# From expert 12 on, down matrices through ScalarE's DMA queue, gate and up together through SyncE's

## The reference

```python
DEPTH = 2; SEQ = 256; D_MODEL = 1024; EXPERT_FF = 512; N_EXPERTS = 32
for l in range(DEPTH):
    h = rms_norm(x, norm_mix[l])
    mix = ...
    x = x + mix
    x = x + hierarchical_moe(rms_norm(x, norm_ffn[l]), ...)
...
def hierarchical_moe(x, ...):
    combine = ...
    for e in range(N_EXPERTS):
        h = jax.nn.silu(t @ w_gate[e]) * (t @ w_up[e])
        out = out + combine[:, e:e + 1] * (h @ w_down[e])
```

## Time and profile before

| what | value |
|---|---|
| median of 3 runs | 1071.91 us (1071.45 to 1071.99) |
| the profiled execution | 1072.4 us, span 1070.7 us |
| PE busy | 809.2 us (76%) |
| DVE, ACT busy | 315.5 us (29%), 194.5 us (18%) |
| HBM read | 437.84 MB, 410 GB/s over the span |
| 36 transfers of 6144 KB | median 33.8 us from issue to landing |

### The profile page before, as it was taken

How to read it: one execution, slowest core, us unless ns; L and a number is a source line. 1 busy time by engine, 2 the same in 40 slices (tenths; PEclk the granted TensorE clock), 3 DMA queues, 4 the chain that set the end, 5 groups by cost and what they waited for, 6 DMA issues and landing times.

```text
span 1070.7 us, 30243 instructions
## 1 busy us (share of the span) xinstructions
PE 809.2 (76%) x13948; PEld 643.4 (60%) x13949; DVE 315.5 (29%) x784; ACT 194.5 (18%) x363; POOL 5.4 (1%) x26
## 2 busy tenths in 40 slices
PE   9999978764867666776899999896456767666675
PEld 9788756543645545555599987564344545545453
DVE  5775522110111111111278744231111111111122
ACT  6784111000000000000254331110000000000002
POOL 1000000000000000000000000000000000000000
PEclk9999999887898888888999989998879888888888
DMA  9979999999999999999998599999999999999995
GB/s 368 425 300 415 388 426 427 428 442 427 428 434 435 424 432 439 433 430 422 418 428 356 218 415 408 425 428 428 439 438 425 422 435 437 433 428 432 441 417 241
DMA packets 26820, 439.94 MB, mean 411 GB/s; under 512 B 3200, under 2 KB 3712, under 8 KB 9088
## 3 DMA queue, kind: packets, MB, share of 16 engines
q1 hardware_dynamic: 26464, 438.36, 96.6%
q10 hardware_dynamic: 288, 0.54, 0.1%
HBM read 437.84 MB, written 1.05 MB: 410 GB/s over the span
## 4 chain that ended last, share of the span: by engine, by line
DMA 53%; PE 41%; issue 4%; DVE 1%; SPq 1%; ACT 1%; DVEq 0%; ACTq 0%
DMA ring<-in_expert_weights 51%; PE psum L1621 12%; PE psum L1409 8%; PE psum L1630 5%; PE psum L1481 4%; PE psum L1638 3%; PE psum L1649 3%; PE psum L1461 2%; DMA ring<-in_even_w_in 2%; PE psum L1644 1%; PE psum L1394 1%; PE psum L1746 1%; PE psum L1381 0%; PE psum L1532 0%; PE psum L1517 0%
## 5 line engine op out<-in xcount | busy, mean ns | idle before, releaser
L1621 PE MATMUL psum<-ring,m 128*32 128x128 f32 x7936 | 299.5, 319 | 225.6 <-DMA ring<-in_expert_weights 201.4
L1621 PEld LDWEIGHTS psum<-ring,m 128*32 128x32 f32 x7936 | 276.1, 130 | 257.8 <-issue 171.9
L1271 DVE TENSOR_TENSOR m<-psum,m 128x128 f32<-128x128 f32 x64 | 18.7, 292 | 544.5 <-ACT m L798 526.9
L1630 PE MATMUL psum<-ring,m 128*32 128x256 f32 x1984 | 120.5, 381 | 3.7 <-DMA ring<-in_expert_weights 3.7
L798 ACT ACTIVATE m<-psum 128x128 f32<-128x128 f32 x60 | 16.7, 278 | 495.2 <-PE psum L1621 495.2
L1409 PE MATMUL psum<-scr_halves,ring_halves 128*128 128x256 f32 x736 | 99.3, 284 | 0.8 <-DVE scr_halves L920 0.6
L1409 PEld LDWEIGHTS psum<-scr_halves,ring_halves 128*128 128x128 f32 x736 | 94.1, 192 | 1.7 <-issue 0.9
L1630 PEld LDWEIGHTS psum<-ring,m 128*32 128x32 f32 x1984 | 64.5, 111 | 49.6 <-issue 5.3
L1638 PE MATMUL psum<-m 32*128 32x256 f32 x1024 | 78.3, 408 | 15.3 <-issue 13.2
L1649 PE MATMUL psum<-x,m 128*32 128x256 f32 x1024 | 73.1, 404 | 1.4 <-issue 1.4
L1638 PEld LDWEIGHTS psum<-m 32*128 32x128 f32 x1024 | 48.1, 186 | 33.3 <-issue 27.6
(11 more groups left out here) (196 smaller groups left out, 518.0 us busy)
## 6 DMA issues: line engine op xcount, KB each, us to landing
ring<-in_expert_weights SPq DMA_DIRECT2D x36, 6144.0 KB, 33.8
ring<-in_expert_weights SPq DMA_DIRECT2D x68, 2048.0 KB, 23.9
ring<-in_expert_weights SPq DMA_DIRECT2D x16, 1024.0 KB, 11.1
ring<-in_odd_w_in SPq DMA_DIRECT2D x5, 2048.0 KB, 26.3
ring<-in_even_w_in SPq DMA_DIRECT2D x3, 2048.0 KB, 22.2
ring<-in_even_w_out SPq DMA_DIRECT2D x2, 2048.0 KB, 31.4
spare<-in_expert_weights SPq DMA_DIRECT2D x2, 2048.0 KB, 21.6
ring<-in_last_down SPq DMA_DIRECT2D x8, 512.0 KB, 32.9
```

The lines of the kernel that those rows point to most:

```text
L1621: last = pe.matmul(GU[CAP * part:CAP * (part + 1), lo:lo + FP], block_of(k), w_of(k)[:, FP * part:FP * (part + 1)], start=k == 0, stop=k = ...
L1630: last = pe.matmul(YB[CAP * part:CAP * (part + 1), 0:DP], h[:, CAP * f:CAP * (f + 1)], w[:, f, DP * part:DP * (part + 1)], start=f == 0, s ...
```

## The change

The transfer of a whole expert is cut in two. SP loads gate and up, 4096 KB, and waits for `gu_ready` of the expert three before, no longer for `y_ready`. ACT issues down, 2048 KB, behind its copy of `yy` of the expert three before; its loop over the turns is cut into four so that only the turns that have a successor to load do so (9 to 14 before `more_experts`, 15 to 26 after it). PE waits for the down matrix before the down product. 18 experts in each of two layers are loaded so.

```diff
--- before.py
+++ after.py
@@ -84,6 +84,7 @@
     for expert in range(FINE):
         if expert != EARLY:
             SINGLE += [entry(layer, expert) + mat for mat in range(3)]
+    SINGLE += [entry(layer, expert) + 2 for expert in range(FINE, NE - 2)]
     SINGLE += [entry(layer, NE - 2) + mat for mat in range(3)]
     SINGLE += [entry(layer, NE - 1) + mat for mat in range(2)]
 SINGLE.append(L_GAIN)
@@ -438,8 +439,9 @@
             def whole(l, e, i, former):
 
                 at = third(l, (i - 1) % TRI)
-                sp.wait_ge(y_ready, after(l, former))
-                sp.dma_start(ring[:, SLOT * 3 * at:SLOT * 3 * (at + 1)], expert_weights_in[l, e]).then_inc(whole_landed[at], 16)
+                sp.wait_ge(gu_ready, after(l, former))
+                sp.dma_start(ring[:, SLOT * 3 * at:SLOT * (3 * at + 2)],
+                             expert_weights_in[l, e][:, 0:2 * SLOT]).then_inc(whole_landed[at], 16)
 
             def turns(l, start, stop):
                 with sp.Fori(start, stop) as b:
@@ -801,6 +803,12 @@
                 act.wait_ge(y_ready, after(l, e))
                 act.activation(yy, YB[:, 0:DP], ACT.Copy).then_inc(yy_ready, 1)
 
+            def load_down(l, e, i):
+
+                n = entry(l, FINE + i) + 2
+                act.dma_start(tall(n), expert_weights_in[l, e][:, 2 * SLOT:3 * SLOT].rearrange("p (j d) -> p j d", j=4)) \
+                    .then_inc(landed[place(n)], 16)
+
             def last_experts(l):
                 for e in LAST_TWO:
                     act.wait_ge(gu_ready, after(l, e))
@@ -821,11 +829,13 @@
                                           scale=rstd[:, t:t + 1])
                 last.then_inc(exps_ready, 1)
                 preload(ACT.Silu)
-                for start, stop in ((0, MIDDLE), (MIDDLE, TURNS)):
+                for start, stop in ((0, ROLLED - 1), (ROLLED - 1, MIDDLE), (MIDDLE, TURNS - 1), (TURNS - 1, TURNS)):
                     with act.Fori(start, stop) as b:
                         for i in range(TRI):
                             expert(l, b * TRI + i)
-                    if start == 0:
+                            if ROLLED - 1 <= start < TURNS - 1:
+                                load_down(l, b * TRI + (i + TRI), i)
+                    if stop == MIDDLE:
                         more_experts(l)
                 last_experts(l)
 
@@ -1715,6 +1725,8 @@
                 def wait_weights(mat):
                     if mat == 0:
                         pe.wait_ge(whole_landed[place(n) // 3], (T + (whole_count(l, FINE + i) - ROLLED)) * 16)
+                    elif mat == 2:
+                        pe.wait_ge(landed[place(n + 2)], (T + (single_count(n + 2) - ROLLED)) * 16)
 
                 expert(l, T * TRI + i, i, wait_weights, lambda mat: lambda k: wide(n + mat)[:, k, :], tall(n + 2))
```

## The result

The changed kernel takes 1073.9 us (median of 15 runs, 1072.15 to 1075.07) against 1070.66 us before (15 runs). The ratio is 1.003 (95% interval 1.0024 to 1.0037), so **3.2 us slower, between 2.6 and 4.0**. Forecast were 2.7 us more. The profiled execution took 1073.53 us, span 1071.8: only 1.1 us above the profiled one of before, because that one (1072.4) was 1.7 above its own median. A single pair of executions can't tell 1 us here; the paces inside the traces tell more.

What follows compares the result with a forecast made beforehand. Weight bytes were taken to bound both expert stages, PE the stretch between. Only the cut had a price, 36 x 0.075 = +2.7 us, all else 0, taking the median from 1071.91 to 1074.6 us, range 1069.3 to 1078.5.

Steps and rivals of the forecast that it cites:

- The bound: Whole kernel: weight bytes set the time in both expert stages, PE between them; DMA share 1.00 from 340 to 480 us.
- The cut, 36 x 0.075 = +2.7 us: Whole-expert loads: each of 36 further transfers costs 0.075 us, a price taken from the experts loaded in three transfers just before.
- Covered gaps: Rival at the whole-expert loads: one queue moves rows while the other closes a transfer; +0.9 us or 0; chance 0.28.
- Better filling: Rival in the steady stretch: two queues fill the engines better, up to 0.1 us per expert, 1068.4 to 1069.7 us; chance 0.14.
- Disturbance: Rival at the DMA engines: rows of two queues interleave and slow each other, +5.4 us, up to +21.6; chance 0.11.
- The dry queue: Rival at PE's first pass through new loop code: queue empties if PE and ACT are over about 10 us later; +3 to +5; chance 0.05.
- the wait for the up product: SP's gate and up loads wait for gu_ready, 4 us sooner in a queue that never runs dry: worth 0.
- ACT's issue: ACT issues down behind its copy of yy: 0.36 us each, covered by 11 us without work, worth 0.
- More code: ACT's four expert loops per layer for two: further code fetches of at most 0.6 to 0.9 us, 0 for the sum.
- PE's wait for down: First matmul of down: one more condition, but the matrix has landed some 30 us before its use; worth 0.
- The order of arrival: Ring: downs overtake queued gate and up, which come up to 9.7 us later, paid back at the stage's end; no cost.

Runs made afterwards that it cites:

- after_again: The changed kernel timed once more, beside new runs of the kernel before: 1073.93 us, 1.0028 against the kernel before.
- after_y_wait: Against the changed kernel, SP waits for y_ready instead of gu_ready before loading gate and up: 1073.64 us, 1.0028 against the kernel before.
- cut_on_sp: Against the kernel before, whole experts load in two transfers (4096 and 2048 KB), both on SP's queue, ACT's program unchanged: 1073.78 against 1070.54 us, 1.0026.
- rows_of_16k: Against the kernel before, padding in HBM splits each 48 KB row into three of 16 KB, still one transfer per expert on SP: 1074.0 us, 1.0035.
- three_on_sp: Against the kernel before, whole experts load in three transfers of 2048 KB, all on SP's queue: 1076.37 us, 1.0048.
- three_two_queues: Against the changed kernel, gate and up are two transfers of 2048 KB on SP, down stays on ACT: 1076.74 us, 1.006 against the kernel before.
- rows_of_8k: Against the kernel before, whole experts load from a padded weight copy, six rows of 8 KB per partition, one transfer: 1085.06 against 1070.3 us, 1.0127.
- whole_two_queues: Against the kernel before, nothing cut, but ACT issues every third whole transfer, with ACT's loops as in the change: 1074.67 us, 1.0037.
- fine9: Against the kernel before, whole transfers start from expert 9 instead of 12: 1069.94 against 1070.43 us, 0.9994; timed again 0.9989.
- fine6: Against the kernel before, whole transfers start from expert 6 instead of 12: 1072.93 us, 1.0021.

## Why the prediction was right, point by point

**The bound** (weight bytes in both expert stages, PE between) stood: share 1.00 and 0.57 in the same windows.

**The cut, 36 x 0.075 = +2.7 us**, was the term that decided, and it came out at 0.072 per expert in the trace, at +3.2 (2.6 to 4.0) in the runs. The pace gives 36 x 0.072 = 2.6 of that; all four timings of a kernel with this cut (+3.2, +3.2 and +3.4, +3.2) lie about 0.6 above it, and what that is made of wasn't found. The prediction took the price from the transfers of 2048 KB in the stage before, and wrote that it makes no difference whether it is per transfer or per row. For the sum that was so; for the steady pace the experiments settle that it is per row:

| kernel | transfers per expert | rows per partition | pace, us |
|---|---|---|---|
| before | 1 | 1 | 14.536 |
| after, after_again, after_y_wait | 2, two queues | 2 | 14.608, 14.609, 14.605 |
| cut_on_sp | 2 | 2 | 14.614 |
| rows_of_16k | 1 | 3 | 14.685 |
| three_on_sp, three_two_queues | 3 | 3 | 14.681, 14.68 |
| rows_of_8k | 1 | 6 | 14.910 |

(14.910 - 14.536) / 5 = 0.075 us per further row. With 128 partitions on 16 engines that is 8 rows an engine, 9.3 ns each. The packets of the profile count these rows: q1 has 26464 before and 49504 in rows_of_8k, 23040 more, which is 36 x 5 x 128. The Trainium skill ("DMA: Bandwidth & Descriptors", Measured) has about 10.5 ns per packet as the floor of a transfer of 4 KB issued by GpSimd; these runs show a cost of about that size, 9.3 ns, for rows of 8 to 32 KB in a full queue. Whether it is the same cost, no run here shows.

**Covered gaps** (the rival of no change) is out: the second queue hid next to nothing, 14.608 against 14.614. **Better filling** is out as well, and the rule of the Trainium skill that is named there ("DMA: Bandwidth & Descriptors", Rules for kernel authors: spreading over issuing engines brings no bandwidth) agrees with that pair. The short intervals on which this rival rested aren't jitter, as the prediction had it: in the kernel before 14.44, 14.62, 14.53 us follow each other in this order from expert 20 of layer two on, one turn of three experts after the other, and the changed kernel has such a pattern too (14.61, 14.52, 14.69). Only a mean over whole turns is a pace; a single interval of 14.44 promised nothing. What the pattern comes from is open. **Disturbance** didn't appear either.

**The dry queue** didn't happen in the changed kernel (0.99). The margin of "about 10 us" was somewhat too wide: in after_y_wait the issue came 10.5 us later and some 2 us of it were idle, so the margin was about 8. The queue ran empty in whole_two_queues too. That the wait for the up product is worth 0 holds for the median. At this one place it put the issue 7 us earlier in the pair of executions above; whether it guards the changed kernel in other executions isn't shown.

**ACT's issue** took 0.344 us for the 0.36 assumed, and nobody waited for it. **More code** cost nothing that can be told: q8 and q14 have their 58 and 10 packets still, and cut_on_sp, without ACT's new loops, takes the same time. **PE's wait for down** cost 0: no matmul of down waited for a DMA in experts 12 to 29 of either layer.

**The order of arrival** is the step that failed, at no cost. "With half of the engines" down was to land in 10 to 15 us; the median was 28.1. And gate products were to be 5 to 10 us late in the middle of the stage; at 398.58 one starts where it was 399.33 before. The changed kernel's ACT issues, and its queues from 355 to 500 us:

```profile
DMA to landing us min/median/max: 13.7/28.1/34.6
```

```profile
q1 hardware_dynamic: 1469, 41.57, 66.6%
q10 hardware_dynamic: 1424, 20.74, 33.6%
```

These numbers alone prove nothing, since gate and up are twice down, in as many rows. But at half of the engines a down would be through in 9.7 us and its queue then empty, while 28.1 us to landing with an issue every 14.6 us means that it always holds work. That fits queues that take turns by row or by groups of as many rows: rows of 32 KB get twice the bytes of rows of 16 KB, and a third of the engines is just what the downs need to keep up, 14.6 us each, so a backlog of two stays, 29 us. With rows of 16 KB on both queues the landing fell to 13.9 us, and the two queues moved as many packets and nearly as many bytes while both had work (three_two_queues), as that account asks. The step that failed is thus the even split by bytes, and a split by rows stands in its place. The overtaking was real only at its start, where SP too had rows of 16 KB: the changed kernel's up product of expert 11 and gate of 12,

```profile
238.40 3.64 PE L1631 MATMUL psum<-ring,m 128*32 128x128 f32 x64 [5.48 <-DMA ring<-in_expert_weights]
...
256.16 6.22 PE L1631 MATMUL psum<-ring,m 128*32 128x128 f32 x127 [8.87 <-DMA ring<-in_expert_weights]
```

came at 238.40 for 231.41 and 256.16 for 250.93. The delay of 5.2 us shrank at once, to 2.3 at expert 14. With the downs not early later on, nothing is paid back at the end in the form forecast: no interval under 11 us between the last whole experts, the shortest in layer two was 13.03 (1017.22 to 1030.25).

## What to carry to other kernels

When the DMA engines are busy all the time, as here, look at bytes and at the length of rows: read the pace between two landings, not the waits, and count the contiguous rows that a cut adds. Making transfers larger pays only as long as the coarser release of their buffers doesn't let the queue run empty once; fine9 and fine6 stand on the two sides of that point. In these runs an earlier wait or a second issuing engine on a full queue moved the time of issue and not the pace of the landings.

## What was not expected of the hardware

- Two full queues shared the DMA engines row for row, so in bytes by their row length: 97 and 100 packets in the same 7 us with rows of 16 KB on both. The same transfer landed in 28.1 us beside rows of 32 KB and in 13.9 us beside rows of 16 KB. Something urgent in short rows beside long ones would come late.
- A further row cost about 9.3 ns on its engine, whether a partition's 48 KB were cut into two, three or six, and whichever transfer or queue the rows were in.
- Executions of one kernel on one chip spread by some 2 to 4 us (before: 1068.41 to 1073.47 in 29 runs), more than the change is worth; the paces in the traces repeated to 0.01 us (14.608 and 14.609).
